# The output projection's first two column groups split by halves, and the value steps and head norms placed later

## What is computed

```python
h = rmsnorm(x, g_pre_mix) * (1.0 + sc1) + sh1
proj = h @ w_in                                   # 2048 -> 6160 (+ a rank-16 gate)
o_sb = rmsnorm(sb_attention(q_sb, k_sb, v_sb))    # 8 heads of 128; samples also read the cache pages
o_g  = rmsnorm(gla(q_g, k_g, v_g, alpha)) * silu(r_g)   # 4 heads of 256, the gated half
out = concatenate([o_sb, o_g], axis=-1) @ w_out   # 2048 -> 2048
x = x + gt1 * rmsnorm(out, g_post_mix)
h = rmsnorm(x, g_pre_ffn) * (1.0 + sc2) + sh2
f = (silu(h @ w_ffn_gate) * (h @ w_ffn_up)) @ w_ffn_down
x = x + gt2 * rmsnorm(f, g_post_ffn)
# sh, sc, gt = six parts of silu(c) @ w_ada + b_ada (2048 -> 12288): the conditioning
```

## Time and profile before

| | |
|---|---|
| median of three runs | 1488.83 us (1487.38 to 1489.83) |
| the profiled execution | 1489.45 us, its span 1487.7 us |
| TensorE matmuls busy | 1428.6 us (96%) |
| TensorE weight loads | 1270.8 us (85%) |
| VectorE busy | 922.3 us (62%) |
| ScalarE busy | 665.3 us (45%) |
| mean granted TensorE clock | 0.983 of full |
| moved by DMA | 396.82 MB, mean 267 GB/s |

### The profile page before, as it was taken

How to read it: one execution, slowest core, us unless ns; L and a number is a source line. 1 busy time by engine, 2 the same in 40 slices (tenths; PEclk the granted TensorE clock), 3 DMA queues, 4 the chain that set the end, 5 groups by cost and what they waited for, 6 DMA issues and landing times.

```text
span 1487.7 us, 29187 instructions
## 1 busy us (share of the span) xinstructions
PE 1428.6 (96%) x11232; PEld 1270.8 (85%) x11232; DVE 922.3 (62%) x1519; ACT 665.3 (45%) x1303; POOL 105.8 (7%) x203
## 2 busy tenths in 40 slices
PE   7779999999899999999999999999999999999997
PEld 2237787887668787796999999999999999999997
DVE  2234588996778667369856766566665675446444
ACT  1023477677655554445543434334344343334333
POOL 0000311113322210000000000000000000200000
PEclk9969999999899999999999999999999999999999
DMA  9999999999999979987666666665666655855552
GB/s 368 421 341 359 388 392 406 379 345 397 392 396 336 342 258 354 404 323 278 221 181 184 178 179 179 181 185 171 183 181 174 185 173 190 233 179 181 182 177 95
DMA packets 139330, 396.82 MB, mean 267 GB/s; under 512 B 13162, under 2 KB 17681, under 8 KB 126433
## 3 DMA queue, kind: packets, MB, share of 16 engines
q1 hardware_dynamic: 117954, 319.59, 63.1%
q0 software_dynamic: 21232, 76.10, 13.5%
q10 hardware_dynamic: 64, 0.07, 0.0%
HBM read 382.28 MB, written 11.34 MB: 265 GB/s over the span
## 4 chain that ended last, share of the span: by engine, by line
PE 84%; DMA 9%; DVE 3%; ACT 2%; issue 1%; POOLq 0%; SPq 0%; POOL 0%; DVEq 0%; ACTq 0%
PE ps L1997 24%; PE ps L1998 24%; PE ps L1999 24%; PE ps L1931 4%; DMA ada_s<-in_w_ada 4%; DMA v_page<-in_cache_v 2%; PE ps L2129 2%; DMA ada_r<-in_w_ada 1%; DMA k_page<-in_cache_k 1%; PE ps L2055 1%; ACT k_page L815 1%; PE ps L1974 0%; DVE k_page L1328 0%; DVE w_lo L1277 0%; ACT w_hi L727 0%
## 5 line engine op out<-in xcount | busy, mean ns | idle before, releaser
L1997 PE MATMUL ps<-h_hi,w_hi 128*128 128x264 f32 x2304 | 666.9, 289 | 6.1 <-DVE h_lo L1265 3.6
L1998 PE MATMUL ps<-h_lo,w_hi 128*128 128x264 f32 x2304 | 658.6, 286 | 0.0
L1999 PE MATMUL ps<-h_hi,w_lo 128*128 128x264 f32 x2304 | 658.2, 286 | 0.0
L1997 PEld LDWEIGHTS ps<-h_hi,w_hi 128*128 128x128 f32 x2304 | 438.1, 190 | 49.1 <-issue 33.6
L1822 DVE TENSOR_TENSOR w_lo<-raw,w_hi 128x1024 fp32r<-128x1024 f32 x254 | 307.2, 1214 | 273.1 <-ACT w_hi L1059 271.7
L1059 ACT ACTIVATE w_hi<-raw 128x1024 fp32r<-128x1024 f32 x264 | 278.5, 1059 | 403.2 <-PE ps L1999 391.0
L1998 PEld LDWEIGHTS ps<-h_lo,w_hi 128*128 128x128 f32 x2304 | 437.4, 190 | 0.5
L1999 PEld LDWEIGHTS ps<-h_hi,w_lo 128*128 128x128 f32 x2304 | 436.3, 189 | 0.0
L1277 DVE TENSOR_TENSOR w_lo<-raw,w_hi 128x1024 fp32r<-128x1024 f32 x138 | 168.8, 1224 | 144.4 <-ACT w_hi L727 143.9
L727 ACT ACTIVATE w_hi<-raw 128x1024 fp32r<-128x1024 f32 x128 | 135.1, 1056 | 174.7 <-PE ps L1999 156.3
L1998 PE MATMUL ps<-act_lo,w_hi 128*128 (+1 forms) x704 | 200.5, 285 | 0.0
(11 more groups left out here) (363 smaller groups left out, 1217.6 us busy)
## 6 DMA issues: line engine op xcount, KB each, us to landing
ada_r<-in_w_ada SPq DMA_DIRECT2D x64, 1024.0 KB, 8.9
raw<-in_w_in SPq DMA_DIRECT2D x96, 512.0 KB, 8.4
raw<-in_w_ffn_gate SPq DMA_DIRECT2D x88, 512.0 KB, 3.7
raw<-in_w_ffn_up SPq DMA_DIRECT2D x88, 512.0 KB, 3.8
raw<-in_w_ffn_down SPq DMA_DIRECT2D x88, 512.0 KB, 4.3
ada_s<-in_w_ada SPq DMA_DIRECT2D x32, 1024.0 KB, 13.2
k_page<-in_cache_k POOLq DMA_DIRECT2D x64, 512.0 KB, 7.9
v_page<-in_cache_v POOLq DMA_DIRECT2D x38, 512.0 KB, 8.0
```

What stands on the lines that cost most here:

```text
L1997: mm(out, w_hi, xh, start=first, stop=False)
L1998: mm(out, w_hi, xl, start=False, stop=False)
L1999: return mm(out, w_lo, xh, start=False, stop=last)
```

## The change

- The 16 units of the first two groups are run in another order: the gated half of group 0 (slots 96 to 99), the gated half of group 1 (100 to 103), the attention half of group 0 (104 to 107), the attention half of group 1 (108 to 111). Groups 2 and 3 stay whole. So there are 18 sets of units between two emptyings of the banks where there were 16.
- After a gated half ScalarE copies the four banks into a new tile `PART`; after an attention half VectorE adds the bank to that copy (`mix_sum`) and ScalarE makes the square and the two copies from the sum (`put_mixed`).
- The value steps go from slots 56 to 92 to slots 56 to 96: steps 0 to 6 stay in their slots, 7 to 15 go from 65 to 74 to 66 to 76 (with slots 65, 70 and 75 free), 16 to 31 from 77 to 92 to 81 to 96. Pages 54 and 59 get a buffer of their own, `VPC`.
- The second half of the heads' norm chain (`put_rows(1)` to `sb_low`) and the conditioning steps 32 to 47 go four slots down, with their loads; the samples' key and value rows three or four; load 48 goes from slot 99 to 114. The first half of the chain for the samples (`dec_rows(0)`, `dec_select(0)`, `put_rows(0)`) goes down by two or three slots, and `dec_select(0)` moves from bank 5 to bank 7. `hx_scale`, `hx_low` and the four gated units stay in slots 94 to 99.

```diff
+        VPC = put("v_page_c", [P, HS], at=at_x + 12800)
+        def vpage(m):
+            if m % 5 == 4 and m >= 54:
+                return VPC
+            return (VPA if m < 32 else VPB)[m % 5]
+        PART = put("mix_part", [P, 2 * MT, T], at=at_h + 8 * T * 4)
...
+        NSET = NIN + NOUT + 2
+        def unit_of(u):
+            if W_OUT <= u < W_OUT + 2 * UPC:
+                part, j = divmod(u - W_OUT, UPC // 2)
+                return NIN + part % 2, j + UPC // 2 * (part // 2)
+            return divmod(u, UPC)
+        def set_of(u):
+            if u < W_OUT:
+                return u // UPC
+            return NIN + (u - W_OUT) // (UPC // 2) if u < W_OUT + 2 * UPC else u // UPC + 2
+        SET_END = {set_of(u): u + 1 for u in range(W_FFN)}
+        SET_AT = {n - 1: e for e, n in SET_END.items()}
+        E_SUM = (NIN + 2, NIN + 3)
...
-            (96, 97, 98, 100, 101, 102, 103, 104, 105, 106, 107, 108, 110, 111, 112, 114))})
+            (100, 101, 102, 104, 105, 106, 107, 108, 109, 110, 111, 112, 114, 115, 116, 118))})
-        A_LOAD.update({32: 94, 33: 95, 34: 98, 38: 101, 39: 102, 48: 99, 49: 101, 51: 113, 52: 116, 53: 118, 54: 120, 55: 121})
+        A_LOAD.update({32: 98, 33: 99, 34: 101, 38: 104, 39: 105, 48: 114, 49: 103, 51: 115, 52: 117, 53: 118, 54: 120, 55: 121})
-        TURN_AT = {20: 2, 55: 3, 115: 4}
+        TURN_AT = {20: 2, 55: 3, 119: 4}
-        AV_SLOT = [56, 57] + [60 + 14 * i // 13 for i in range(14)] + [77 + i for i in range(16)]
+        AV_SLOT = [56, 57] + [60 + 16 * i // 13 for i in range(14)] + [81 + i for i in range(16)]
-        DROW_AT = {75: 0, 93: 1}
+        DROW_AT = {77: 0, 97: 1}
-        MIX_AT = {8 * (NIN + 1 + gi) + 1: gi for gi in range(NOUT - 1)}
-        XG_AT = {110: 0, 114: 1, 122: 2}
+        MIX_AT = {109: 0, 113: 1, 121: 2}
+        XG_AT = {112: 0, 114: 1, 122: 2}
...
+                if m == 54:
+                    pool.wait_ge(dec_mm, 24)
...
+            def put_mixed(src, gi, m):
+                k = gi * MT + m
+                s.activation(SQD[:, m if gi == 0 else 4 + m, :], src, ACT.Square)
+                s.activation(MT_[:, k, 0:TP], src[:, 0:TP], ACT.Copy, scale=scale_t[:, k, 0:1])
+                return s.activation(MT_[:, k, TP:T], src[:, TP:T], ACT.Copy)
+            def evac(e, m):
+                if e in E_SUM:
+                    gi = e - NIN - 2
+                    act.wait_ge(bank_out, MT * e + m + 1)
...
+                    put_mixed(PART[:, MT * gi + m, :], gi, m).then_inc(mix_put, 1)
+                    return
...
+                elif e < NIN + 2:
+                    s.activation(PART[:, MT * (e - NIN) + m, :], ps[:, m, 0:T], ACT.Copy).then_inc(bank_out, 1)
+                else:
+                    if m == 0:
+                        act.wait_ge(acc_ready, 1)
+                    put_mixed(ps[:, m, 0:T], e - NIN - 2, m).then_inc(bank_out, 1)
...
             def hx_low(h):
                 dve.wait_ge(norm_hi, h + 1)
+                dve.wait_ge(av_used, 30)
...
+            def mix_sum(e, m):
+                if m < 3:
+                    dve.wait_ge(bank_done, 3 * e + m + 1)
+                else:
+                    dve.wait_ge(unit_used, SET_END[e])
+                part = PART[:, MT * (e - NIN - 2) + m, :]
+                v.tensor_tensor(part, part, ps[:, m, 0:T], ALU.add).then_inc(bank_out, 1)
...
-                if st == 76:
+                if st == 79:
                     put_rows(0)
...
-                if st == 95:
+                if st == 99:
                     put_rows(1)
                     head_squares(0)
+                if st == 95:
                     hx_scale(1, 5)
                     hx_scale(2, 6)
                     hx_low(0)
+                if st == 100:
+                    sb_root(0, 4)
...
+                if st in SET_AT and SET_AT[st] in E_SUM:
+                    for m in range(3):
+                        mix_sum(SET_AT[st], m)
...
                 elif v == 16:
-                    pe.wait_ge(dout_ready, 1)
+                    pe.wait_ge(d_put, 1)
...
-                if st == 75:
-                    pe.wait_ge(kt_ready, 1)
-                    dec_select(0, 5)
+                if st == 78:
+                    dec_select(0, 7)
...
-                    pe.wait_ge(sb_oev, 2)
-                    sb_means(0, 4)
...
+                if st == 98:
+                    dec_select(1, 7)
+                if st == 99:
+                    pe.wait_ge(sb_oev, 2)
+                    sb_means(0, 4)
+                if st == 100:
+                    pe.wait_ge(norm_rs, 2)
+                    rstd_bcast(0, 4)
+                if st == 101:
                     pe.wait_ge(norm_h, GH + 1)
                     rstd_bcast(1, 4)
```

More of the change, by code:

```diff
@@ L454, in _ @@
                             sp.wait_ge(av_used, n - 1)
+                        if n == 48:
+                            sp.wait_ge(mix_put, MIX_PUT0 + 2 * MT)
                         if n == 34:
@@ L594, in v_page @@
                 page = pool.value_load(PT[0:1, m:m + 1], min_val=0, max_val=NPOOL - 1)
-                pool.dma_start((VPA if m < 32 else VPB)[m % 5][:, :],
+                pool.dma_start(vpage(m)[:, :],
                                pool_v[bass.ds(page, 1), :, :].rearrange("o p n -> p (o n)")).then_inc(vpage_in[m % 5], 16)
@@ L727, in hi @@
                 s.activation(HI[:, u % 4, :], RAW[:, u % 4, :], ACT.Copy).then_inc(hi_ready, 1)
-            def evac(g, m):
+            def put_mixed(src, gi, m):
[7 more added lines that the diff above has]
+                    act.wait_ge(bank_out, MT * e + m + 1)
+                    if gi == 0 and m == 0:
+                        act.wait_ge(scl_ready, 1)
+                    put_mixed(PART[:, MT * gi + m, :], gi, m).then_inc(mix_put, 1)
+                    return
@@ L730, in evac @@
                 if m < 3:
-                    act.wait_ge(bank_done, 3 * g + m + 1)
+                    act.wait_ge(bank_done, 3 * e + m + 1)
                 else:
[L733 to L748, removed]
+                    act.wait_ge(unit_used, SET_END[e])
+                if e < NIN:
+                    s.activation(unit_dst(e, m), ps[:, m, 0:T], ACT.Copy).then_inc(bank_out, 1)
+                elif e < NIN + 2:
[4 more added lines that the diff above has]
+                    put_mixed(ps[:, m, 0:T], e - NIN - 2, m).then_inc(bank_out, 1)
@@ L749, in evac_frees @@
+            def evac_frees(e):
+                if e == 4:
                     act.wait_ge(g_scan, GH * TB)
-                if g == 6:
+                if e == 6:
                     act.wait_ge(t_mask, 8)
-                if g == 7:
+                if e == 7:
                     act.wait_ge(k_even, 25)
                     act.wait_ge(k_odd, 25)
-                if g == 9:
+                if e == 9:
                     act.wait_ge(av_used, 16)
-                if g == 8:
+                if e == 8:
@@ L922, in _ @@
             for st in range(NSLOT):
-                if st % UPC == 0 and st > 0:
-                    evac(st // UPC - 1, 3)
+                if st - 1 in SET_AT:
+                    evac(SET_AT[st - 1], 3)
                 if 0 < st < NSLOT - 3:
@@ L995, in _ @@
                     dec_logs(1)
-                if st == 76:
-                    for b in range(4, 8):
-                        dec_probs(b)
                 if st in SILU_AT:
@@ L1008, in _ @@
                     dec_rows(DROW_AT[st])
+                if st == 77:
+                    for b in range(4, 8):
+                        dec_probs(b)
                 if st - 1 in SB_AT:
@@ L1035, in _ @@
                     sb_result(3, 5)
-                if st == 99:
+                if st == 103:
                     sb_high(0)
-                if st == 100:
+                if st == 104:
                     rs_heads(1, 5)
                     sb_high(1)
-                if st == 101:
+                if st == 105:
                     sb_high(2)
@@ L1050, in _ @@
                     rs(rstd[0:64, :], rvar[0:64, :], 2)
[L1051 to L1054, removed]
+                if st in SET_AT:
+                    evac_frees(SET_AT[st])
+                    for m in range(3 if SET_AT[st] < NSET - 1 else 0):
+                        evac(SET_AT[st], m)
             def hi_n(nb, u):
@@ L1456, in put_rows @@
                 even, odd = (bass.AP(tensor=src.tensor, offset=src.offset, ap=[src.ap[0], [36, 2], [P + 1, 4], [H, 4]])
-                             for src in (ps[:, 5 if x == 0 else 7, 0:512], ps[:, 5 if x == 0 else 7, 64:512]))
+                             for src in (ps[:, 7, 0:512], ps[:, 7, 64:512]))
                 link(v.tensor_copy(dst, even))
@@ L1666, in slot @@
                     sb_low(3)
-                if st == 103:
+                if st == 107:
                     kv_row(0, 4)
                     kv_row(1, 6)
-                if st == 106:
+                if st == 109:
                     kv_row(2, 5)
@@ L1678, in slot @@
```

(18 more changed lines are left out.)

68 lines of the change are left out of this document (34 added, 34 removed).

## The result

The changed kernel takes 1495.88 us (median of 8 runs, 1494.63 to 1498.64), the kernel before 1490.03 us in the same runs: ratio 1.0041, 95% interval 1.0029 to 1.0052. It is slower by 0.41%, some 6 us; the forecast was +2.7 us, and the measured time lies 0.9 us above the stated range. (1.2 us of the distance is the starting point: the forecast stood on a median of 1488.83 us from three runs.) The profiled execution took 1498.64 us, its span 1497.0 us, so its waits are on the large side; a second one, of 1493.79 us, stands among the experiments.

What follows compares the result with a forecast made beforehand. TensorE was taken to bound the kernel from 420 us, DMA engines also full, with slot 68 held by VectorE's late row. Terms 1.1 - 1.8 + 2.0 + 1.4 - 0.4 + 0 + 0.4 = +2.7 us: median 1491.5 us, own range 1490 to 1494, overall 1484.5 to 1495.

Steps and rivals of the forecast that it cites:

- term 7: Slots 109 to 118: conditioning loads meet fuller queues, some come late, row stores are small; +0.4 us, bounds 0 and 4.
- terms 1 to 3: Slots 65 to 68, +1.1 us; slots 69 to 76, -1.8 us; half clock after the long wait, +2.0 us.
- terms 4 to 6: Slots 77 to 80 without value steps, +1.4 us; slots 93 to 103, -0.4 us; the halves' copies and adds hidden, 0.
- a sign of being wrong: Among the signs against the forecast: TensorE waits for `ada_r` in slots 114 to 118; no size given.
- late conditioning loads as a rival: Loads 46 and 47 land 4 us late, TensorE waits in slots 116 and 118; 1495.1 us, chance 0.10.
- The faster rival: Last key page lands before VectorE is ready at 410.1 us, waits stay away; -5.0 us, 1483.9 us, chance 0.18.
- Terms 4 and 5: Slots 77 to 80: waits at two heads' sums, +1.4 us; slots 93 to 103: one wait goes, part returns, -0.4 us.

Runs made afterwards that it cites:

- old first half: The changed kernel with value steps 2 to 15 back in their old slots (60 to 74); ratio 1.0025 to the kernel before.
- early store: The changed kernel with GpSimd's 1 MB store of the value rows put ahead of its key-row stores; ratio 1.0025 to the kernel before.
- old first half + early store: The changed kernel with value steps 2 to 15 in their old slots and the value-row store ahead of the key-row stores; ratio 1.0009 to the kernel before.
- product 62 in slot 68: The changed kernel with VectorE's product with key page 62 one slot later, behind the state rows TensorE waits for; ratio 0.9996 to the kernel before.
- late loads: The changed kernel with conditioning loads 48 and 51 to 55 asked for in SP's slots 119 to 123 instead of 114 to 121; ratio 1.0024 to the kernel before.

## Why the prediction was wrong

By pairs of ratios, in us of 1490; each carries about 2 us of uncertainty.

| terms | forecast | measured | from |
|---|---|---|---|
| 1 to 3, first half and clock | +1.3 | +2.4 | change less old first half; the same with early store |
| 4 to 6, slots 77 to 103 and halves | +1.0 | +1.3 | old first half + early store |
| 7, conditioning loads | +0.4 | +2.4 | change less early store |
| sum | +2.7 | +6.1 | measured +6.1 |

Of the 3.4 us between forecast and measurement, 2.0 us belong to term 7, 1.1 us to terms 1 to 3 and 0.3 us to terms 4 to 6, so far as the uncertainty lets one divide them.

**The step that failed is term 7.** It said that GpSimd's row stores "move four slots with their rows and are small". The rows are; but a store of 1 MB stands behind them in the same order and moved with them, into the transfer of the old x and in front of loads 42 and 43. By the traces the term is 3.5 us in the profiled execution of the change and 1.4 to 1.6 us in its second one and in two kernels with the same store and loads (old first half, product 62 in slot 68): units 110 to 125, less the 52.63 us without waits. The rest of that step's working fits what was found: more bytes than the time carries, and load 47 late in slot 118, which was named as a sign of being wrong. (With 1 MB as 1.05 million bytes its 18.5 MB are 18.9 MB.) Load 42, late in slot 111, it didn't name.

I had priced late conditioning loads as a rival, 1495.1 us with a chance of 0.10, just outside my own range. That the measured time comes near it is chance: the rival had waits of 3.6 us in slots 116 and 118, the two executions of the change have 2.8 and 0.8 us, most of it in slots 111 and 119, and terms 1 to 3 add their own miss. The store was overlooked because I looked for what was new in SyncE's queue and not for what a waiting instruction on GpSimd held back. The Trainium skill (DMA: Bandwidth & Descriptors, Queues, rings and completion order) says that a DMA engine takes its queues in turn, packet by packet. The runs show the sharing, not the turns: the store stands on GpSimd's queue and the loads on SyncE's, and load 42 took 17.5 and 13.9 us in the two executions of the change, 11.4 us without the store.

**Terms 1 to 3: the mechanism was right, the size was not.** One wait in slot 68 released by `state_rows` (forecast 5.5 us, found 6.1 and 6.3), half clock behind it, no value-page wait after slot 68 up to slot 76: all found. Two sizes were off. I held the page's landing for fixed; counted from the end of unit 64, TensorE got the row after 23.0 us before and after 25.1 and 24.9 us in the two executions. The page took 12.0 and 12.1 us instead of 10.6 us, and it was issued 0.7 and 0.4 us later by this count, as the value step of slot 64 waited for its own page, which it hadn't before:

```profile
398.44 1.06 PE L2192 MATMUL ps<-v_page,a_dec 128*32 128x512 f32 x8 [1.56 <-DMA v_page<-in_cache_v]
```

```profile
397.79 1.06 PE L2129 MATMUL ps<-v_page,a_dec 128*32 128x512 f32 x8
```

And from the row to the end of unit 69 it is 7.3 us instead of 4.6 us, 2.7 us for the clock where I took 2.0 us. Why the page took longer is open, and it need not be the spread: in seven traces without it the page took 10.6 to 11.9 us, in seven with it 11.4 to 12.1 us.

One reading of mine was wrong without harm to the sum: of the six value-page waits in the earlier trace rows two lie in slots 56 to 64 (2.23 and 3.22 us), not three; the other four are those that I list.

**The faster rival** named the landing of the page as its condition. The runs show a better one: VectorE's order. The page was as late in the kernel with product 62 moved, and the gain came all the same.

**Terms 4 and 5** are close: 0.41 and 0.33 us at the first two heads' sums (0.7 each was forecast), 0.8 us at the head means of slot 99 (0.7), none in slot 95.

On the rule by which one improves first the engine with the highest occupancy, or for DMA the highest HBM utilization (the Trainium skill, Perfetto Trace Analysis, Identifying the Most-Contended Engine): by the ratios, relieving the DMA engines lost 2.4 us and gained 4.0 us with the same transfers, depending on what stood in front of a row on VectorE. Here the wait that ended last decided, not which engine was fullest.

## What to carry to other kernels

Before thinning out one wait, walk the stage forward on every engine and ask who is next and what stands in front of it in that engine's order: a product that nobody needs yet, in front of a row that TensorE needs, turned a gain of 4.0 us into a loss of 2.4 us (by the traces 1.8 and 3.7 us), and moving it by one slot turned it back. When a step moves, list everything that is queued behind it on its issuing engine with its bytes, not only what the step itself issues.

## What the runs showed of the hardware

After nearly the same wait in slot 68 (6.1 to 6.3 us) the granted clock stayed at half for 6.8 us in both executions of the change and for 10.2 us in the kernels with the early store and with the late loads. In the latter two it fell 3.6 and 3.8 us before the wait ended, in the two executions of the change 0.8 and 1.0 us, so most of the difference cost nothing: from the row to the end of unit 69 they took 7.6 and 7.5 us, the change 7.3 and 7.2 us.

In the profiled execution of the change a conditioning load of 1 MB issued between 570 and 690 us took between 4.7 us (35) and 17.5 us (42). Ahead of load 42 a load of 2.1 MB and a store of 1 MB had been issued within 3.3 us.
